# Last layer's forget and query features of three head pairs by the seven-product scheme, with three joined smaller changes

## What is computed

```python
def hgrn2_layer(h, w_in, b_in, lb, head_norm, w_out):
    proj = h @ w_in + b_in                      # (512, 1024) @ (1024, 4096)
    fp, iv, qp, z = jnp.split(proj, 4, axis=-1)
    logf = jnp.log(lb + (1.0 - lb) * jax.nn.sigmoid(fp))
    k = (1.0 - lb) * jax.nn.sigmoid(-fp)
    q = jax.nn.silu(qp)
    o = hgrn2_chunkwise(heads(q, HGRN_HEADS), heads(k, HGRN_HEADS), heads(iv, HGRN_HEADS), heads(logf, HGRN_HEADS))
    o = rms_norm_2(...)                         # per head
    return (o * jax.nn.silu(z)) @ w_out
```

## Time and profile before

| | us |
|---|---|
| median of 3 runs | 1665.08 |
| lowest, highest | 1664.26, 1665.38 |
| the profiled execution | 1664.51 |
| its span, first to last instruction | 1662.5 |
| TensorE busy (matrix products) | 1648.2, 99% |
| VectorE busy | 909.3, 55% |
| ScalarE busy | 383.9, 23% |
| GpSimd busy | 208.6, 13% |

### The profile page before, as it was taken

One profiled execution on the slowest core, in us unless ns is written; L12 is line 12 of the kernel. 1 busy time (PEld: TensorE's weight loads), 2 busy tenths in 40 slices (PEclk: granted clock), 3 DMA queues, 4 the chain that ended last, 5 costly groups with the idle time before them and its releaser, 6 DMA issues.

```text
span 1662.5 us, 20384 instructions
## 1 busy us (share of the span) xinstructions
PE 1648.2 (99%) x7899; PEld 1034.9 (62%) x7899; DVE 909.3 (55%) x1528; ACT 383.9 (23%) x686; POOL 208.6 (13%) x267
## 2 busy tenths in 40 slices
PE   9999999999999999999999999999999999999999
PEld 5887888885534333343435886688866654667664
DVE  3755746674523232232325876777756645667663
ACT  3112212001200001000002121331145524544530
POOL 2333410001100000000001100000225510000000
PEclk9999999999999999999999999999999999999999
DMA  7313113245899999999998014213220022112101
GB/s 286 122 62 121 51 52 136 102 158 208 311 417 426 429 425 426 427 426 428 426 428 344 29 61 156 73 58 138 99 102 1 2 76 91 61 51 97 56 1 51
DMA packets 28003, 308.14 MB, mean 185 GB/s; under 512 B 4415, under 2 KB 4703, under 8 KB 10112
## 3 DMA queue, kind: packets, MB, share of 16 engines
q1 hardware_dynamic: 21456, 288.70, 42.8%
q0 software_dynamic: 6448, 18.10, 3.1%
HBM read 306.06 MB, written 4.19 MB: 187 GB/s over the span
## 4 chain that ended last, share of the span: by engine, by line
PE 96%; DVE 3%; POOL 0%; issue 0%; ACT 0%; DVEq 0%; ACTq 0%
PE ps L463 90%; PE ps L466 5%; DVE arena L1367 2%; DVE arena L1378 0%; POOL small L3155 0%; DVE small L1382 0%; ACT arena L2699 0%; DVE H L1367 0%; ACT HT L2699 0%; DVE arena L1372 0%; DVE arena L1394 0%; DVE wring L1367 0%; DVE arena L1382 0%; DVE HT L1394 0%; POOL small L3153 0%
## 5 line engine op out<-in xcount | busy, mean ns | idle before, releaser
L463 PE MATMUL ps<-arena 128*64 128x512 f32 (+12 forms) x2516 | 536.2, 394 | 1.6 <-DVE arena L1390 1.2
L463 PEld LDWEIGHTS ps<-arena 128*64 128x64 f32 (+4 forms) x2516 | 257.4, 157 | 218.7 <-issue 208.4
L463 PE MATMUL ps<-wring,arena 128*64 128x512 f32 (+3 forms) x1208 | 369.7, 534 | 0.5 <-ACT arena L2699 0.5
L1367 DVE TENSOR_TENSOR arena<-ps,arena 128x512 f32<-128x512 f32 (+1 forms) x209 | 143.2, 685 | 360.7 <-PE ps L463 206.3
L463 PE MATMUL ps<-wring,HT 128*128 128x256 f32 (+1 forms) x784 | 248.9, 468 | 3.1 <-ACT HT L2699 2.4
L463 PE MATMUL ps<-HT,wring 128*128 128x512 f32 (+2 forms) x656 | 223.2, 502 | 0.0
L2699 ACT ACTIVATE arena<-ps 128x512 f32<-128x512 f32 (+4 forms) x146 | 81.5, 558 | 601.2 <-PE ps L466 312.7
L463 PEld LDWEIGHTS ps<-wring,arena 128*64 128x64 f32 (+1 forms) x1208 | 153.1, 153 | 90.9 <-issue 83.6
L463 PE MATMUL ps<-wring 128*128 128x256 f32 x912 | 206.5, 380 | 0.0
L463 PEld LDWEIGHTS ps<-wring,HT 128*128 128x128 f32 x784 | 145.4, 190 | 81.0 <-issue 68.2
L463 PEld LDWEIGHTS ps<-wring 128*128 128x128 f32 x912 | 171.2, 190 | 25.1 <-issue 2.6
(11 more groups left out here) (128 smaller groups left out, 1041.0 us busy)
## 6 DMA issues: line engine op xcount, KB each, us to landing
wring<-in_w SPq DMA_DIRECT2D x47, 2048.0 KB, 20.9
wring<-in_dense SPq DMA_DIRECT2D x38, 2048.0 KB, 8.3
arena<-in_w SPq DMA_DIRECT2D x35, 2048.0 KB, 19.9
HT<-in_w SPq DMA_DIRECT2D x12, 2048.0 KB, 17.5
arena<-in_rows POOLq DMA_DIRECT2D x29, 256.0 KB, 3.9
wring<-in_dense SPq DMA_DIRECT2D x2, 1024.0 KB, 5.8
H<-in_x SPq DMA_DIRECT2D x4, 512.0 KB, 6.9
arena<-in_relb POOLq DMA_DIRECT2D x8, 256.0 KB, 8.9
```

Source lines behind the costliest of these rows:

```text
L463: return nc.tensor.matmul(o, l, r, start=start, stop=stop, skip_group_check=True)
L1367: done(nc.vector.tensor_tensor(o, a, b, op), tell)
```

## The change

- For p = 1 to 3 the x projection goes by seven products too, apart for the forget and the query features (`FEATURES`): 4 products in group 0 (2), 3 in group 1 (3). Each bank X, Y, Z holds two products and W one, so each is read out when full. VectorE makes T1 to T3 of both in `feature_sums`, during the turn before, and adds up the products in `features(p, g, part)`. The features then lie in SBUF, and ScalarE's sigmoids read them there, the query ones into a tile of their own. The row sums are needed one projection sooner.
- The order of VectorE's and ScalarE's work in a turn changes, as shown.
- The scaling of the keys by `lb1` on VectorE becomes a bias (its logarithm) of ScalarE's exponentials.
- `o_y0` goes by seven products (`product`, with the sums in `take`, `sum_t23` and so on), and `o_x0` is made in two halves of the tokens, the first ones ahead of the last transpositions.
- Smaller ones: in `softmax_a` query tiles 2 and 0 of a head pair share an item and a bank (12 items instead of 16, 4.76 pieces a step instead of 3.76); the second half of `m_q`'s first product comes ahead of `turn("D", 2)`; `n_z`'s last two products come ahead of `turn_out(2)` and `turn_out(3)`, and the first filler of `softmax_d` ahead of the wait for `kcT` and the first scores.

```diff
+FEATURES = ((1, "A11", "B11", "X", 0), (3, "S2", "T2", "X", 1), (4, "S1", "T1", "Y", 0), (5, "S4", "B22", "Y", 1),
+    (6, "S3", "T3", "Z", 0), (2, "A12", "B21", "Z", 1), (7, "A22", "T4", "W", 0))
+SUMS_X = {3: 1, 4: 2, 7: 3}
...
-LANE = {"w_pg0": ("sumh", 8, "tookm", 16), "w_pg1": ("sumg", 0, "tookg", 0), "m_v": ("sumh", 11, "tookm", 19), "m_q": ("sumh", 14, "tookm", 22)}
+LANE = {"w_pg0": ("sumh", 8, "tookm", 16), "w_pg1": ("sumg", 0, "tookg", 0), "m_v": ("sumh", 11, "tookm", 19), "m_q": ("sumh", 14, "tookm", 22),
+"o_y0": ("sumh", 17, "tookm", 25)}
+SUMH_X = 20
+TOOKM_X = 28
+ROWS_HAD = {"C": 5, "D": 7, "E": 9}
...
+def of_features(key, g):
+    w = wslot[PLACE[key][0]].rearrange("p (i k g j n) -> p i k g j n", i=2, k=4, g=2, j=2)
+    sumX = nbs[0].rearrange("p (k g n) -> p k g n", k=4, g=2)
+    sumY = pj[:, 1, :].rearrange("p (k g n) -> p k g n", k=4, g=2)
+    q = dict(B11=w[:, 0, :, :, 1], B12=w[:, 0, :, :, 0], B21=w[:, 1, :, :, 1], B22=w[:, 1, :, :, 0], T1=sumY, T2=sumX)
+    q.update(T3=q["B12"], T4=q["B11"])
+    return {n: x if g is None else x[:, :, g] for n, x in q.items()}
...
-            yield dict(x=8 * hh + 2 * (3, 0, 2, 1).index(q), hh=hh, q=q, nk=128 * (q + 1), last=q == 1)
+        for n, qs in enumerate(((3,), (2, 0), (1,))):
+            o, own = 0, []
+            for q in qs:
+                own.append(dict(q=q, o=o, nk=128 * (q + 1), y=8 * hh + 2 * (3, 2, 0, 1).index(q)))
+                o += 128 * (q + 1)
+            yield dict(x=6 * hh + 2 * n, hh=hh, parts=own, nk=o, first=n == 0, last=n == 2)
...
-FILL_A = softmax_slots(("u", "cg", "bg", "ga0", "ga1"), lambda g: 14, 3.76, NIA + 3)
+FILL_A = softmax_slots(("u", "cg", "bg", "ga0", "ga1"), lambda g: 14, 4.76, NIA + 3)
...
+        filling(0)
+        evacuated(("nqT", 2), ("nqT", 3), ("nkT", 2), ("nkT", 3), "kcT")
         for i in range(NIT + 3):
             if i < NIT:
                 score(ITEMS[i])
-            filling(2 * i)
+            if i:
...
-        product("m_q", 1, (0,))
+        product("m_q", 1)
         turn("D", 2)
-        product("m_q", 1, (1,))
         product("m_q", 2, (0,))
...
+        seventh("n_z", 12)
+        seventh("n_z", 13)
         for i in (2, 3):
             turn_out(i)
-        seventh("n_z", 12)
...
-            if i > 1:
-                turn("E", i - 2)
+            if i == 2:
+                turn("E", 0)
...
+        def features(n, half):
+            f = F["fx", 0, n] if half else fill(("fx", 0, n))
+            w = weight("o_x0")
+            t = slice(256 * half, 256 * half + 256)
+            for k in range(8):
+                ins = mm(f.ap[:, t], w[:, k * 512 + n * 128:k * 512 + n * 128 + 128], HT[:, k, t], not half and k == 0,
+                         half == 1 and k == 7)
+            if half:
+                ins.then_inc(f.full, 1)
+                used["o_x0"] = f
         def group(p, n):
             if n < 4:
-                used[f"o_x{p}"] = feat(("fx", p, n), weight(f"o_x{p}"), n * 128)
-            elif p:
+                g = n // 2
+                if not n:
+                    weight(f"o_x{p}")
+                for m, x, y, bank, half in FEATURES[4:] if n % 2 else FEATURES[:4]:
+                    name = ("fx", p, g, bank)
+                    f = F[name] if half else fill(name)
+                    if m in SUMS_X:
+                        pe.wait_ge(S("sumh"), SUMH_X + 4 * (p - 1) + SUMS_X[m] + (m == 7 and g))
+                    a, b = of_rows("last")[x], of_features(f"o_x{p}", g)[y]
+                    for k in range(4):
+                        ins = mm(f.ap[:, 256 * half:256 * half + 256], b[:, k], a[:, k, :], not half and not k, k == 3)
+                    if half or m == 7:
+                        ins.then_inc(f.full, 1)
+                    used[f"o_x{p}"] = f
+            else:
                 for s in range(2):
                     seventh(f"o_y{p}", 2 * n - 8 + s)
...
-        for n in (4, 5, 6, 7, 0, 1, 2, 3):
-            group(0, n)
+        among(2, 3)
+        product("o_y0", 1, (0,))
+        turn("E", 1)
+        product("o_y0", 2, (0,))
+        for n in (1, 2):
+            product("o_y0", n, (1,))
+        among(4, 5)
+        turn("E", 2)
+        among(6)
+        features(0, 0)
+        among(2, 3)
+        turn("E", 3)
+        among(7, 4, 5)
+        for n in (1, 2, 3):
+            features(n, 0)
+        for i in (2, 3):
+            turned("E", i)
+        for n in range(4):
+            features(n, 1)
+        for n in (3, 4, 6, 5):
+            product("o_y0", n)
+        among(0, 1)
         step(0, "scores", 0)
+        product("o_y0", 7)
+        every.i, now[0] = spot[0] + 4, every
         for p in range(1, 4):
             for n in range(11):
-                if (p, n) == (1, 5):
-                    pe.wait_ge(S("suma"), 10)
+                if (p, n) == (1, 0):
+                    pe.wait_ge(S("suma"), 11)
...
         def queries(p, c):
             x, q = 2 * p + c, pQ[p % 2][:, c, :]
             heard("qs")
-            f = F["fx", p, 2 + c]
-            stt(q, f.ap, PC("b_qp")[:, x:x + 1], q, ADD, MUL, f)
+            if p:
+                stt(q, q, PC("b_qp")[:, x:x + 1], qsig[:, c, :], ADD, MUL)
+            else:
+                f = F["fx", p, 2 + c]
+                stt(q, f.ap, PC("b_qp")[:, x:x + 1], q, ADD, MUL, f)
+        def feature_sums(p):
+            w, (s, n, _) = of_features(f"o_x{p}", None), PLACE[f"o_x{p}"]
+            v.wait_ge(S(f"w{s}"), 16 * n)
+            tt(w["T3"], w["B22"], w["B12"], SUB)
+            tt(w["T2"], w["T3"], w["B11"], ADD, "sumh")
+            tt(w["T1"], w["B22"], w["T2"], SUB, "sumh")
+        def features(p, g, part):
+            w = of_features(f"o_x{p}", g)
+            fx = {b: F["fx", p, g, b] for b in "XYZW"}
+            h = {b: [f.ap[:, 256 * x:256 * x + 256] for x in range(2)] for b, f in fx.items()}
+            d = (pB, pQ)[g][p % 2]
+            c11, c21, c12, c22 = d[:, 1, 0:256], d[:, 1, 256:512], d[:, 0, 0:256], d[:, 0, 256:512]
+            four = pj[:, 2, 0:256]
+            if part == 0:
+                full("fx", p, g, "X")
+                copy(c11, h["X"][0])
+                tt(c21, h["X"][1], c11, ADD, fx["X"])
+                tt(w["T4"], w["B21"], w["T2"], SUB, "sumh")
+                full("fx", p, g, "Y")
+                tt(four, h["Y"][0], c21, ADD)
+                tt(c12, h["Y"][1], four, ADD, fx["Y"])
+            elif part == 1:
+                full("fx", p, g, "Z")
+                tt(c22, h["Z"][0], four, ADD, "tookm")
+                tt(c11, h["Z"][1], c11, ADD)
+                tt(c21, h["Z"][0], c21, ADD, fx["Z"])
+            else:
+                full("fx", p, g, "W")
+                tt(c21, h["W"][0], c21, ADD, fx["W"])
...
-                freed(("fx", p, c))
-                ts(kk, kk, lb1[:, x:x + 1], None, MUL)
...
-        r = row("b_ivz")
-        for i in range(4):
-            if i:
-                gated(i - 1)
-            f = full("ty", i)
-            tt(pvz[0][:, i, :], f.ap, r[1], ADD, f)
-            if i in (0, 2):
-                turned("E", 2 + i // 2)
-            if i == 2:
-                for j in range(4):
-                    freed(("t", "E", j, 0))
-                sums_of_rows("last")
+        r, to = row("b_ivz"), behind(pvz[0])
+        for i in (2, 3):
+            turned("E", i)
+        for j in range(4):
+            freed(("t", "E", j, 0))
+        rows_12("last")
+        take("o_y0", 1, to, by_row(r))
         row_done(r)
-        gated(3)
-        z_gain(0)
+        take("o_y0", 2, to, by_row(r))
+        sum_t23("o_y0")
+        sum_t1("o_y0")
+        rows_34("last")
         prep(0, 0, 0)
         prep(0, 0, 1)
         heard("eE", 3)
         for x in ("keys", "blocks", "state"):
             prep(0, 0, x)
+        take("o_y0", 3, to, by_row(r))
+        sum_t4("o_y0")
         queries(0, 0)
         prep(0, 0, "queries")
         prep(0, 0, "out")
         queries(0, 1)
+        for n in (4, 6):
+            take("o_y0", n, to, by_row(r))
+        z_half(0, 1)
+        take("o_y0", 5, to, by_row(r))
         scores(0, 0)
         prep(0, 1, 0)
+        feature_sums(1)
+        take("o_y0", 7, to, by_row(r))
+        z_half(0, 0)
+        z_gain(0)
         for p in range(1, 4):
             y, r = f"o_y{p}", row("b_ivz" + "+" * p)
             prep(p - 1, 1, 1)
+            features(p, 0, 0)
             states(p - 1, 0)
-            for x in range(3):
-                weighed(p - 1, 1, x)
+            weighed(p - 1, 1, 0)
+            features(p, 0, 1)
+            weighed(p - 1, 1, 1)
+            weighed(p - 1, 1, 2)
+            features(p, 0, 2)
             sums_of_weight(y)
+            features(p, 1, 0)
+            scores(p - 1, 1)
+            features(p, 1, 1)
+            prep(p, 0, 0)
+            features(p, 1, 2)
+            prep(p, 0, 1)
             queries(p, 0)
-            scores(p - 1, 1)
-            prep(p, 0, 0)
             queries(p, 1)
-            prep(p, 0, 1)
```

(36 more changed lines are left out.)

114 lines of the change are left out of this document (56 added, 58 removed), and 2 rows, old and new, of the table SPOT.

## The result

The changed kernel takes 1676.01 us (median of 6 runs, 1674.01 to 1678.82) against 1664.65 us before (6 runs on the same chip): a ratio of 1.0069, 95% interval 1.0056 to 1.0081. It is slower by 11.4 us where 2.4 were forecast, and above the range. All times are device time; a ratio is that of the medians, after over before, both on one chip.

A forecast was written before the change was run, and what follows sets the result against it. TensorE, busy 1648 of 1662.5 us, was taken as the bound. From 1664.5 us, savings of 20.0 and added waits and half clock of 22.8 gave 1667.3, put down as 1667.5 us; range 1660 to 1673.

The forecast's parts named there:

- VectorE's 54 us: VectorE's work in each loop turn rises from 43.1 to 54 us, leaving next to no room.
- the half clock: After each turn's long TensorE wait the clock halves for 3.41 us, losing 1.7 us, 5.1 over three turns.
- T2: In each turn TensorE waits 0.75 us for this feature-weight sum, 2.3 us over three turns.
- The wait: TensorE idles 4.55 us ahead of each turn's second `outs`, behind a late ScalarE sigmoid: 13.65 us in all.
- The table switch: On ScalarE, between powers and second query sigmoid, a table load takes 1.39 us, as in the earlier trace.
- Rival D: Each ScalarE table switch costs a drain besides, 1.28 us three times on the chain: 1671.1 us; chance 0.04.
- T4 and `states`: In turns 2 and 3 the forget product's T4 comes 0.55 us late and `states` 0.3: 1.7 us.
- TensorE's saving in the loop: Features by seven half-size products save TensorE 3.3 us per pair of heads, 10.0 us over three pairs.
- Ahead of the loop: Gains from the opening (5.4 us) and three smaller changes (2.5, 1.0 and 1.1 us).
- `n_z`: Two products moved ahead of the turning at 1213.70 fill its idle time: 1.0 us gain, 0 if `kcT`'s copy isn't done.
- The opening: Last layer's start until the first pair's scores falls from 62.20 to 56.8 us: 5.4 us gain.
- Rival C: VectorE does not catch up within a turn, late at query bank Z: 2 us a turn, 1673.2 us; chance 0.18.

The follow-up runs named there:

- x4_old_loop: The changed kernel with the three turns put back as before the change, key powers keeping their bias operand, opening and smaller changes kept: 1655.77 us, ratio 0.9952.
- the fillers: The changed kernel with 5 useless matmuls in each turn's idle time, 1671.56 us; likewise with four weight sums left out, 1663.99 us against 1668.68 without matmuls.
- w4_after_again: The changed kernel run once more, with nothing altered: 1676.59 us, ratio 1.0069.
- x1_sigmoid_first: The changed kernel with ScalarE's second query sigmoids ahead of the first chunk's powers instead of behind them: 1660.97 us, ratio 0.9979.
- v1_first_bank_early: The changed kernel with powers, states and weight sums earlier, queries spread, and bank X and T4 taken at the end of the turn before: 1652.62 us, ratio 0.9932.
- w2_powers_first: The changed kernel with VectorE's scan and subtractions ahead of collecting the third query bank, and ScalarE's powers ahead of both query sigmoids: 1667.91 us, ratio 1.0019.
- x2_states_first: The changed kernel with VectorE's second-chunk states ahead of the two query products that wait for the late sigmoid: 1671.43 us, ratio 1.0045.

## Why the prediction was right and wrong

**Right:** the sign, and the mechanism with its place (`outs` behind `states` behind `queries` behind the sigmoid behind the powers); when TensorE would want `outs` (9.3 us after bank Z, as forecast); VectorE's 54 us; the half clock; the places of the small waits. T2 came out at 0.77 us a turn for 0.75 (the terms named there make 0.7: 5.9 less 5.2).

**Wrong:** the sizes. The sum had +2.8 us on the profiled execution; the span grew by 10.2.

- The wait, 13.65 forecast, 15.7 measured (3 x 5.24). In the walk the powers started at 5.57 and not 5.37 after bank Z, took 4.79 and not 4.51 us, and the steps behind added 0.2. The powers got longer through the change itself: three of them now have a bias operand. With the old loop and the bias kept (`x4_old_loop`) they take 4.79 us too. I had carried the old row over. The Trainium skill (ScalarE: Activation LUTs, What ACT_TABLE_LOAD costs) gives about 93 ns for each pointer operand, by which three would add an estimated 0.28 us; the trace agrees, 4.79 against 4.51.
- The table switch, 1.39 us in the earlier trace rows: 1.37 measured from the powers' end (1440.18) to the sigmoid's start. Rival D had no part.
- T4 and `states` (the waits ahead of the first chunk's `outs`), 1.7 forecast, 3.5 measured start to start: 0.66 us in the first turn, where I had none, 1.59 in the second and 1.25 in the third. T4 alone came 1.17 and 0.83 us late in those two, for 0.55.
- The half clock, 5.1 forecast: 6.7 lost by the trace (three stretches in which TensorE works 13.35 us), some 5 in the medians of the fillers. I took 3.41 us for each stretch; two were 6.83, and in the profile of `w4_after_again`, the same kernel, all three.
- TensorE's saving in the loop, 10.0 forecast, 9.4 measured (3 x 3.12). With T2's 2.3 these make 15.7 + 2.3 + 3.5 + 6.7 - 9.4 = +18.8, which is what the loop grew by; forecast 12.8.
- Ahead of the loop, -10.0 forecast, -8.6 measured. `n_z` gave next to nothing for 1.0: I named that copy, and it is what TensorE stands for. The opening gave 4.3 for 5.4, most of the difference in the wait where I had 0.3 us of room.

So the step that failed is the sizing of the terms of the sum, on a chain that had no slack. Together they were some 7.4 us short: 2.1 in the wait, 1.8 in T4 and `states`, 1.6 in the half clock, 0.6 in TensorE's saving and 1.4 ahead of the loop. No single one of them would take the time out of the range. Rival C's time (2 us a turn above the forecast) is near where the total came out, but its mechanism was not this one: at bank Z of the queries, where VectorE was to be late, it still waits 0.85 us for TensorE (the row at 1430.02), and the large wait stays without the 5.1 us of sums.

## What to carry to other kernels

A product saved on the busy engine pays only if the order of the engines behind it is rebuilt with it: here the same products made the kernel 11 us slower or 11 us faster than before, and of the second 8.3 us came from the other parts of the change. Ask of each long wait that costs nothing now what hides it, and check every engine's order for work that is ready but stands behind a result that isn't. When the helper engine gets near nine tenths of the turn (54.0 of 59.9 us here), half of the change may give as much as all of it. Look up what a change does to the instructions on the chain itself, here the bias operands, before their old durations are carried over.

## What I had not expected of the hardware

- A stretch at half clock of 3.41 us starts at about 1064 us in the profiled executions of 11 of the 18 kernels run (`w4_after_again`, `x1_sigmoid_first`), near thin matmuls of four rows, with no idle time over 0.6 us before it. In others (`x4_old_loop`) it is missing, and so it is in the first profile of the changed kernel, the same program as `w4_after_again`: it depends on the execution. It fits two groups of times of one kernel: `v1_first_bank_early` took 1654.07 us in the profiled execution, which has it, and 1652.3 to 1652.8 in the four with a mean clock of 1.000. That these lack it isn't shown, since only one was profiled. Medians of five that differ by under 2 us may differ by this alone.
- An idle time of 3.38 us brought half clock in one of three turns (`w2_powers_first`), 3.96 in all three (`x2_states_first`), 1.36 in none (`x1_sigmoid_first`).
- Three exponentials with a bias operand cost 0.28 us more together.
